# Six query and key tiles of the forget heads moved among the gate tiles of attention's ticks, with aligned stage buffers

## What is computed

```python
def hybrid_mixer(h, w_in, ...):
    (q_a, k_a, v_a, f_a, q_b, k_b, v_b, q_c, c_kv, q_i, k_i, w_i, gates) = jnp.split(h @ w_in, ...)
    y_a = forgetting_attention(heads(q_a, 6), heads(k_a, 6), heads(v_a, 6), f_a + b_forget)
    y_b = stick_breaking_attention(heads(q_b, 5), heads(k_b, 5), heads(v_b, 5))
    ...
    y_c = dsa_attention(q_c, k_c, v_c, q_i, k_i, w_i)     # picks the 64 best keys by an index score
    g_a, g_b, g_c = jnp.split(jax.nn.sigmoid(gates), 3, axis=-1)
    return (g_a * (y_a @ w_up_fox) + g_b * (y_b @ w_up_sb) + g_c * (y_c @ w_up_dsa)) @ w_out

for l in range(2):
    x = x + 0.5 * swiglu(rmsnorm(x, ...)); x = x + hybrid_mixer(rmsnorm(x, ...)); x = x + 0.5 * swiglu(...)
```

## Time and profile before

| | |
|---|---|
| median of 3 runs | 2031.75 us (2031.67 to 2032.75) |
| the profiled execution, its own time | 2032.25 us |
| its span, first to last instruction | 2030.6 us |
| PE busy | 1960.0 us (97%) |
| DVE busy | 1526.7 us (75%) |
| ACT busy | 1031.0 us (51%) |
| mean granted PE clock | 0.996 |

### The profile page before, as it was taken

One profiled execution on the slowest core, in us unless ns is written; L12 is line 12 of the kernel. 1 busy time (PEld: TensorE's weight loads), 2 busy tenths in 40 slices (PEclk: granted clock), 3 DMA queues, 4 the chain that ended last, 5 costly groups with the idle time before them and its releaser, 6 DMA issues.

```text
span 2030.6 us, 32702 instructions
## 1 busy us (share of the span) xinstructions
PE 1960.0 (97%) x11980; PEld 1718.1 (85%) x11980; DVE 1526.7 (75%) x2637; ACT 1031.0 (51%) x1582; POOL 44.9 (2%) x80
## 2 busy tenths in 40 slices
PE   7999999999999999999899999999999999999998
PEld 6888898988888888899888888888788888887887
DVE  7887567579888987657678887785767778667766
ACT  5445545654446444545565445566444455555443
POOL 0000000000000000000000000000000000000000
PEclk9999999999999999999999999999999999999999
DMA  7874543257774876453246774441455544233553
GB/s 298 293 283 172 190 156 131 88 180 280 277 268 153 287 281 215 167 186 125 94 169 247 282 250 150 170 149 71 145 186 186 186 179 173 95 125 135 186 186 135
DMA packets 77286, 382.18 MB, mean 188 GB/s; under 512 B 9296, under 2 KB 9472, under 8 KB 55936
## 3 DMA queue, kind: packets, MB, share of 16 engines
q1 hardware_dynamic: 67392, 329.78, 44.9%
q0 software_dynamic: 9792, 51.00, 7.6%
HBM read 379.65 MB, written 1.10 MB: 188 GB/s over the span
## 4 chain that ended last, share of the span: by engine, by line
PE 82%; DVE 9%; ACT 6%; issue 3%; DMA 1%; SPq 0%; DVEq 0%; ACTq 0%
PE psum L674 21%; PE psum L585 15%; PE psum L586 15%; PE psum L587 15%; PE psum L677 11%; DVE weights_low_a L1446 2%; ACT weights_high_a L1069 1%; PE psum L883 1%; ACT x_normed L1077 1%; PE psum L821 1%; PE psum L812 1%; PE psum L910 1%; PE psum L911 1%; PE psum L909 1%; DMA raw_a<-in_w_ffn_a_a 1%
## 5 line engine op out<-in xcount | busy, mean ns | idle before, releaser
L674 PE MATMUL psum<-h_high_low,weights_high_a 128*128 128x512 f32 x1840 | 654.7, 398 | 5.4 <-DVE h_high_low L1491 3.3
L1446 DVE TENSOR_TENSOR weights_low_a<-raw_a,weights_high_a 128x2048 fp32r<-128x2048 f32 (+1 forms) x232 | 459.8, 1983 | 123.2 <-ACT weights_high_a L1069 121.2
L677 PE MATMUL psum<-h_high_low,weights_low_a 128*128 128x256 f32 x1840 | 514.2, 279 | 0.0
L674 PEld LDWEIGHTS psum<-h_high_low,weights_high_a 128*128 128x128 f32 x1840 | 345.3, 188 | 92.5 <-issue 5.3
L1069 ACT ACTIVATE weights_high_a<-raw_a 128x2048 fp32r<-128x2048 f32 (+1 forms) x232 | 386.0, 1664 | 65.1 <-PE psum L587 61.4
L677 PEld LDWEIGHTS psum<-h_high_low,weights_low_a 128*128 128x128 f32 x1840 | 346.7, 188 | 6.6 <-issue 1.0
L1446 DVE TENSOR_TENSOR weights_low_b<-raw_b,weights_high_b 128x1024 fp32r<-128x1024 f32 x224 | 273.3, 1220 | 54.5 <-ACT weights_high_b L1069 54.0
L1069 ACT ACTIVATE weights_high_b<-raw_b 128x1024 fp32r<-128x1024 f32 x224 | 235.4, 1052 | 104.6 <-PE psum L587 104.6
L1139 ACT ACTIVATE up_low_products<-psum 128x512 f32<-128x512 f32 (+1 forms) x146 | 74.1, 507 | 391.7 <-PE psum L677 391.6
L585 PE MATMUL psum<-weights_high_b,gated_high 128*128 128x512 f32 x608 | 241.8, 398 | 4.6 <-DVE gated_low L1575 2.8
L587 PE MATMUL psum<-weights_high_b,gated_low 128*128 128x512 f32 x608 | 241.3, 397 | 0.0
(11 more groups left out here) (300 smaller groups left out, 3165.9 us busy)
## 6 DMA issues: line engine op xcount, KB each, us to landing
ada_weights<-in_w_ada POOLq DMA_DIRECT2D x64, 768.0 KB, 5.9
raw_a<-in_w_ffn_a_a SPq DMA_DIRECT2D x44, 1024.0 KB, 7.3
raw_a<-in_w_ffn_b_a SPq DMA_DIRECT2D x44, 1024.0 KB, 7.4
raw_a<-in_w_ffn_a SPq DMA_DIRECT2D x64, 512.0 KB, 4.4
raw_b<-in_w_ffn_b SPq DMA_DIRECT2D x64, 512.0 KB, 3.3
raw_a<-in_w_proj_a SPq DMA_DIRECT2D x28, 1024.0 KB, 5.5
raw_a<-in_w_gate_a SPq DMA_DIRECT2D x26, 1024.0 KB, 4.8
raw_b<-in_w_ffn_a_b SPq DMA_DIRECT2D x44, 512.0 KB, 3.9
```

Of the source, the lines that this page charges most:

```text
L674: pe.matmul(ps[:, bank, :], whi[0][:, p, c:c + P], hboth[:, k, :, :].rearrange("p a b -> p (a b)"), start=k == 0, stop=False, skip_group_c ...
L677: last_mm = pe.matmul(ps[:, bank, SEQ:2 * SEQ], wlo[0][:, p, c:c + P], hhi[:, k, :], start=False, stop=k == KD - 1, skip_group_check=True)
L1446: dve.tensor_tensor(wlo[kind][:, p, 0:width], raw[kind][:, p, 0:width], whi[kind][:, p, 0:width].bitcast(F32), ALU.subtract).then_inc(lo_r ...
```

## The change

- The weights of q and k of the fox heads are taken out of the start of the turned tiles and put behind those of the sb heads (`w1_late`). `project_turned` makes 6 tiles (two slots), q and k of sb.
- The ticks now hand out 30 tiles: the 6 of the fox heads first (`QK_LATE`), then the 24 gate tiles. They begin at slot `FF1 + 6`. The table gives one tile to each of the ticks 0 to 26 and a second one to ticks 15, 18 and 20. Ticks 17, 19 and 23 no longer go without.
- DVE's token work is arranged anew about the two slots that are left, and two small memsets move from the end of it to its start.
- `mid` is rounded up to a multiple of 128 bytes (32 bytes further), and `gated_high` and `gated_low` go to a place of their own at a multiple of 512.

```diff
-GATE_TICKS = {1: [t for t in range(27) if t not in (17, 19, 23)],
+GATE_TICKS = {1: list(range(16)) + [15, 16, 17, 18, 18, 19, 20, 20, 21, 22, 23, 24, 25, 26],
...
+def gates_of(blk, tick):
+
+    return [g for g, at in enumerate(GATE_TICKS[blk]) if at == tick]
...
-        mid = at[0]
+        mid = at[0] = (at[0] + 127) // 128 * 128
+        apart = (mid + 74752 + 511) // 512 * 512
...
+        ghi = put("gated_high", [P, 2, SEQ], F32R, apart)
+        glo = put("gated_low", [P, 2, SEQ], F32R, apart + 2048)
...
                 if kind == "fox":
+                    pe.wait_ge(now().gate_copied, QK_LATE)
                     pe.wait_ge(now().forget_rows_ready, 2)
...
-                    g = gate_of(blk, tick)
-                    if g is not None:
+                    for g in gates_of(blk, tick):
                         gate_tile(l, blk, walk, g)
...
-                        project_turned(l, 1, Walk(SLOTS1, FF1 + 4, 4, KD, 4), 12, 8)
+                        project_turned(l, 1, Walk(SLOTS1, FF1 + 4, 2, KD, 4), QK_EARLY, 8)
-                        ticks(l, 1, schedule1(), 24, Walk(SLOTS1, FF1 + 8, 8, KD, 0))
+                        ticks(l, 1, schedule1(), QK_LATE + 24, Walk(SLOTS1, FILL1, FILL_SLOTS1, KD, 0))
...
             def projections1(l):
+                chain.also(dve.memset(y1[:, :, 384 + SB * HD:768], 0.0))
+                chain.also(dve.memset(y1[:, :, 768 + DSA * HD:YT1 * P], 0.0))
                 row_splits(l, 1, FF1, 0)
                 row_splits(l, 1, FF1, 1)
-                for n, work in enumerate((tokens1, tokens1_forget, tokens1_index, tokens1_queries), FF1 + 4):
-                    split_low(l, 1, 1, n + 1)
-                    split_low(l, 1, 0, n + 2)
-                    work()
+                split_low(l, 1, 1, FF1 + 5)
+                tokens1()
+                split_low(l, 1, 0, FF1 + 6)
+                split_low(l, 1, 1, FF1 + 6)
+                tokens1_forget()
+                tokens1_index()
+                split_low(l, 1, 0, FF1 + 7)
+                tokens1_queries()
```

More of the change, by code:

```diff
@@ L314, in build @@
         fa = put("gated", [P, SEQ], F32, mid + 12288)
-        ghi = put("gated_high", [P, 2, SEQ], F32R, mid + 13312)
-        glo = put("gated_low", [P, 2, SEQ], F32R, mid + 15360)
+        ghi = put("gated_high", [P, 2, SEQ], F32R, apart)
+        glo = put("gated_low", [P, 2, SEQ], F32R, apart + 2048)
         ada_w = put("ada_weights", [P, 2, KD // 2, ADA], F32, mid + 17408)
@@ L914, in ticks @@
             def ticks(l, blk, items, gates, walk):
-                pe.wait_ge(now().proj_copied, 20 if blk == 1 else 12)
+                pe.wait_ge(now().proj_copied, 8 + QK_EARLY if blk == 1 else 12)
                 if blk == 2:
@@ L1181, in project_turned @@
             def project_turned(l, blk, n0, groups_before):
-                w = Walk(SL[blk], n0, 4, KD, groups_before)
-                for g in range(12):
+                w = Walk(SL[blk], n0, 2, KD, groups_before)
+                for g in range(QK_EARLY):
                     s, m = g // 3, g % 3
@@ L1289, in gate_tile @@
                 act.wait_ge({"a": now().used[0], "b": now().used[1], "g": now().group_done}[mark[0]], mark[1])
-                act.activation((g1 if blk == 1 else g2)[:, g, :], ps[:, g % 2, 0:SEQ],
-                               ACT.Copy).then_inc(now().gate_copied, 1)
+                late = QK_LATE if blk == 1 else 0
+                if g < late:
+                    out, scale = qk1[:, g // 3, g % 3, :], SCALE if g < 3 else 1.0
+                else:
+                    out, scale = (g1 if blk == 1 else g2)[:, g - late, :], 1.0
+                act.activation(out, ps[:, g % 2, 0:SEQ], ACT.Copy, scale=scale).then_inc(now().gate_copied, 1)
             def gate_tanh(blk, f):
@@ L1302, in ticks @@
                 for tick in range(len(items) + TURN_LAG + 1):
-                    g = gate_of(blk, tick)
                     item_copy(blk, items, tick - TURN_LAG - 1)
                     stick_exp(items, tick - 1)
-                    if g is not None and g % 3 == 0:
-                        split_high(l, blk, 1, n0 + g // 3 + 1)
                     if tick in TOKEN_WORK_ACT[blk]:
                         TOKEN_WORK_ACT[blk][tick]()
-                    if g is not None:
+                    for g in gates_of(blk, tick):
+                        if g % 3 == 0:
+                            split_high(l, blk, 1, n0 + g // 3 + 1)
                         gate_tile(blk, walk, g)
@@ L1764, in ticks @@
                 for tick in range(len(items) + TURN_LAG + 2):
-                    g, before = gate_of(blk, tick), gate_of(blk, tick - 1)
                     item_late(items, tick - 1)
@@ L1771, in ticks @@
                     item_y(blk, items, tick - TURN_LAG - 2)
-                    if g is not None and g % 3 == 0:
-                        split_low(l, blk, 1, n0 + g // 3 + 1)
-                    if before is not None and before % 3 == 1 and before < gates - 2:
-                        split_low(l, blk, 0, n0 + before // 3 + 2)
+                    for g in gates_of(blk, tick):
+                        if g % 3 == 0:
+                            split_low(l, blk, 1, n0 + g // 3 + 1)
+                    for g in gates_of(blk, tick - 1):
+                        if g % 3 == 1 and g < gates - 2:
+                            split_low(l, blk, 0, n0 + g // 3 + 2)
                     if tick in TOKEN_WORK[blk]:
@@ L2060, in _ @@
                         projections1(l)
-                        chain(dve.memset(y1[:, :, 384 + SB * HD:768], 0.0))
-                        chain(dve.memset(y1[:, :, 768 + DSA * HD:YT1 * P], 0.0))
-                        ticks(l, 1, schedule1(), 24, FF1 + 8)
+                        ticks(l, 1, schedule1(), QK_LATE + 24, FILL1)
                         turn_y(Y_EARLY, YT1)
```

23 lines of the change are left out of this document (12 added, 11 removed).

## The result

| | before | after |
|---|---|---|
| median | 2032.25 us (4 runs, 2031.67 to 2035.27) | 2015.83 us (4 runs, 2014.99 to 2016.28) |
| span of the profiled execution | 2030.6 us | 2014.6 us |
| PE busy | 1960.0 us | 1951.8 us |
| mean granted PE clock | 0.996 | 0.998 |

The ratio is 0.9915, with an interval from 0.990 to 0.993. The kernel is 16.4 us faster. So the direction and most of the size are right, and 3.5 us of the gain are not in the sum. PE's busy time fell by 8.2 us although it does the same 11980 matmuls; matmuls at half the clock, and slower ones, count as busy for longer.

The account below looks back on a forecast made before the run. PE, busy 1960.0 of 2030.6 us, was taken as the bound, so only waits and slow clock could be won: -7.5 - 1.8 - 3.6 = -12.9 us, stated as 2018.9 us (-0.63%). The range was 2016.4 to 2024.5 us.

Parts of the forecast that it names:

- the sum: Whole kernel: long wait, short wait and slow clock together save 12.9 us, for a forecast of 2018.9 us, chance 0.76.
- The moved tiles: Six turned tiles leave the stretch before the ticks (17.3 us less) and enter the ticks (17.3 us more); net 0.
- The long wait: Tick 19, ahead of the values of fox head 1: PE's 3.73 us wait goes in both layers, -7.5 us.
- the short one: First block's ticks: PE's wait behind `negated_row_max`, once in each layer, goes, -1.8 us.
- The slow clock: Matmuls after the tick 19 wait no longer run slowed: 2.0 us in layer 0, 1.6 in layer 1, -3.6 us.
- Rivals A and B: A: up to two new waits per layer, 2022.9 us, chance 0.10; B: nothing won, about 2031.7 us, chance 0.07.
- Late next: Second tiles in ticks 15, 18, 20 add 5 DVE splits; tightest has 4.7 us to spare: 0, upper bound +4.
- rival C: DVE finishes part a of tick 21's slot so late that PE stands longer; slower, for instance 2039.4 us; chance 0.04.
- The token work: Before tick 0, six tiles less cover, yet DVE's result comes with 6.4 us to spare: 0.
- The addresses: Matmuls on unaligned `y_high` and aligned `h_high_low` both take 2.88 us per 24, so alignment costs PE 0.
- rival D: Down projections: aligned `gated_high` and `gated_low` make matmuls 2% faster, a further -8.8 us, 2010.1 us; chance 0.03.
- `x_normed`: PE waits 9.1 us in all for this buffer, which moves; a tenth allowed either way, 0.9 us.

## Why the prediction was right or wrong, point by point

- **The moved tiles, net 0**: right. The stretch ahead of the ticks lost 17.28 us where 6 x 2.88 = 17.3 was said.
- **The long wait, -7.5, the short one, -1.8**: right. Both are gone in both layers, also with the tiles only. The walk by DVE's durations met the trace within 0.4 us in the six places that were compared (the seventh was set equal).
- **The slow clock, -3.6**: right in kind, and by size within the scatter. Filling the wait gave 2.95 us; by the trace 2.2 in layer 0 and 1.6 in layer 1, where 2.0 and 1.6 were said. The same wait has a slow stretch of 3.4 us in some executions and of 6.8 in others (in layer 0 6.8 before, 3.4 with `mid` rounded), so the 3.6 is the price of one execution.
- **Their sum, -12.9**: the tiles only gave -13.05, and by the interval of their ratio 10.8 to 16.3, so that the last digits agree is luck. The traces before and after differ by 13.8 in the mixers. Of the 0.9 more, 0.3 are the two long waits counted from start to start and 0.2 the slow clock of layer 0; the range had allowed 0.7 for the former. Rivals A and B are out: no new wait came, and the waits of ticks 3 and 4 stayed at 4.0 us.
- **Late next and rival C**: didn't happen here, but its mechanism is real. It appeared, at 3.85 us, when the same tiles were paired in ticks 4 to 9.
- **The token work, 0**: right. The first matmuls of tick 0 carry no wait for tokens, only the same 0.52 us before the first of them as before.
- **The addresses, 0**: this is the step that failed. Because 24 matmuls on `y_high` and 24 on `h_high_low` both take 2.88 us, it said "No difference, so 0." The comparison was of other tiles in another stage, on 256 columns, and took a property of one address as if it were one of alignment in general. The runs show 2.808 against 2.782 us for 12 down matmuls, 3.9 us in a kernel, of which the gate and up matmuls give 0.9 to 1.1 back: -2.8 to -3.0 by the traces, -3.1 by the memory edits alone, -3.7 between the tiles only and the changed kernel, the last two with some 2 us of uncertainty. That is rival D's case with 0.9% in place of its 2% and a chance of 0.03. A changed pace in the feed-forward was also among the prediction's own signs of being wrong. With 2% it had -8.8 us, and the range was cut off between the two: its low end had 0.9 us for the addresses, for another matter (`x_normed`), so it couldn't hold a third of D's price. The bounds for a cost that no row shows must take in the nearest row from both sides, and here both bounds were put equal to the one comparison.
- **`x_normed`, up to 0.9 us either way**: 10.5 us in 15 waits in the trace after, 9.2 in 14 in the repeat of the changed kernel. It varies by a single wait with the same addresses, and so says nothing of them.

## What to carry to other kernels

When waits of the engine that bounds the kernel come from another engine's short backlog, move work of the bounding engine into just those ticks: the six tiles gave -13 us with the additional work in ticks 15 to 23, and +10 with it in ticks 4 to 9, although that kernel also has the memory edits, worth about -3. Walk the late engine tick by tick with durations from its timeline; that met the trace within 0.4 us here. And where an edit moves a buffer that matmuls read, don't set it to 0 because another pair of buffers shows no difference: a kernel with thousands of matmuls should be given about 1% of the time of that stage's matmuls, either way, for the means of those that read the buffer moved by up to 1.8% here and of those that don't by 0.9%. And compare means over many groups, not one group with one.

## What the runs showed of the hardware

- The pace of back-to-back matmuls changes with the place of operands in memory. Eight arrangements of two tiles of 2 KB gave means of 2.758 to 2.808 us for 12 matmuls of 512 columns that load them as weights, and of 5.596 to 5.645 us for 32 matmuls between these that don't read them. The time of the kernel moved by 5.7 us (2015.58 to 2021.23).
- The 32 matmuls take either 5.55 or 5.64 us, nothing between, in two repeating patterns; an arrangement changes how many groups are long, from 36 of 76 to all.
- The remainder by 128 doesn't set it. Where several kernels share an arrangement (two did), they repeat its pace of the down matmuls within 0.001 us.
- PE kept at matmuls through a gap of 3.7 us kept its clock at 1.00, and was 2.2 us earlier at the same point of layer 0 than with the gap.
